# Nine gather buffers for each expert table, in memory shared with the second block's constants

## The chip, the core and the metric

The kernel runs on one core of a Trainium2 chip. The metric is the device time of one execution, in microseconds. The core has a matrix engine (TensorE, PE), a vector engine (VectorE, DVE), an activation engine (ScalarE, ACT), GpSimd (POOL), which here does nothing but issue the gathers, and SyncE (SP), which issues the plain loads. All transfers run on the same 16 DMA engines.

## What is computed

A sequence of 256 tokens and 16 meta tokens, 1024 wide, goes through a first block of two layers, and then through a second block with three attention branches and a feed-forward network. What matters here is the expert layer (`peer`), which each of the first two layers ends with. For every token it picks 128 experts (8 heads, top 16 of each), and every expert is one row of 1024 numbers in each of two tables of 16,384 rows:

```python
u_sel = jnp.take(u, expert, axis=0)
v_sel = jnp.take(v, expert, axis=0)
act = jax.nn.gelu(jnp.einsum('btd,bthkd->bthk', hx, u_sel), approximate=False)
return jnp.einsum('bthk,bthkd->btd', (gate * act).astype(h.dtype), v_sel)
```

The second block's constants (rotary cosines and sines, a swap and a flip matrix, the decay of the retention branch, the bucket and mask rows of the relative bias) come as one array `cs2` of 128 x 3584 numbers.

## The kernel before, in words

Tokens lie on the 128 partitions, in tiles: tile 0, tile 1, and tile 2 with the 16 meta tokens. The expert layer of a tile is a row of **slots**. In slot k every partition (token) gets its k-th expert: GpSimd issues one gather of 128 rows of `peer_u` (L344, 512 KB) and then one of 128 rows of `peer_v` (L349, 512 KB). There are 528 slots: 16 for the meta tokens, in which the eight heads lie on the partitions, and 128 each for tile 0 and tile 1 of the first layer and tile 0 and tile 1 of the second. Number them n = 0 to 527.

What a slot goes through, in order:

- VectorE multiplies the `u` row by the token's row and sums (`dot`, L1435, semaphore `dot`).
- ScalarE takes the gelu of the 128 sums (`gelu`, L932).
- VectorE makes a 128x128 diagonal matrix of gelu times gate (`coef`, L1444, semaphore `diag`, four buffers). In its instruction order it comes two slots behind the dot. It waits until TensorE has done slot n-4.
- TensorE multiplies the diagonal by the `v` row and adds it up in two banks of PSUM (`sums_slot`, L494, four matmul records a slot). It raises the semaphore `vsum`.

A `u` gather of slot n waits in GpSimd's queue until dot n-NU is done, a `v` gather until the sum of slot n-NV is done. NU is 4 and NV is 8. As GpSimd issues u(n), v(n), u(n+1), ... in one queue, a gather that waits holds back all that follow. The buffers lie in one tile `a1` of 12 x 1024 numbers a partition, the `u` buffers in front.

The order of the other work around the slots is written out by hand. `Beside.to(n)` on TensorE, ScalarE and VectorE means: first do the slots up to n, then go on. The tables `PLAN` (the two `front` passes) and `SIDE` say at which slot each piece of other work comes. `topk` finds the experts of a tile (about 230 steps on VectorE) and writes their numbers to `eidx` (L1424), for which GpSimd waits at each tile. The slots of one tile run beside the next tile's projections, attention and top-k:

- slots 16 to 143 (layer 0, tile 0), 228 to about 604 us, beside the rest of the first layer's top-k; from about 400 us nothing else runs but slots (the straight stretch);
- slots 144 to 271, to about 1110 us, beside `front(0)`: projections, attention (`stick`, eight steps), output projection, query projection, top-k;
- slots 272 to 399, to about 1600 us, beside `front(1)`, the same for tile 1;
- slots 400 to 527, to about 1974 us, beside the second block's first steps (`SIDE`): the memory tokens' keys and values, the bias rows (`trev`, `flip`); from about 1740 us nearly nothing but slots.

After the last slot the second block begins (`split_cols_unit`, L652). The matrices `swap` (L747) and `decayed` use `cs2c`, the buffer of `cs2`.

SyncE loads the weights in 270 units of 512 KB into a ring of R = 8, each when the unit eight back has been used. In this queue stand, before, the loads of `cs2c`, `bcG` and `tsb` ahead of unit `wqA`, and, ahead of unit SPLIT0 (the second block's first with the split weights), a wait for the last top-k and the loads of `mem` and of the last gain row.

Of the kernel before, what the change touches and what calls it, by code (L numbers as in the profile page):

```python
# [22 lines left out]
R = 8  # L23
NU = 4
NV = 8
# [53 lines left out]
CS2 = {}  # L79
# [5 lines left out]
NCS2 = _at  # L85


def program(nc, xin, metain, units, cols, cst, cs2, poolm, bc_rows, peer_u, peer_v, mem, rel, out):
# [10 lines left out]
    with ctx:  # L99
        def sb(name, shape, dt=fp32):  # L100
            return ctx.enter_context(nc.sbuf_tensor(name, shape, dt))
# [33 lines left out]
        A1W = (NU + NV) * 1024  # L135
# [11 lines left out]
        vg = a1[:, NU * 1024:A1W].rearrange("p (n d) -> p n d", d=1024)  # L147
# [54 lines left out]
        cs2c = sb("cs2c", [128, NCS2])  # L202
        bcG = sb("bcG", [128, 512])
        tsb = sb("tsb", [128, 32])
        oh2 = sb("rot_tmp", [128, 512])
# [20 lines left out]
        memx = pw  # L226
        up_cv = a2[:, pw_at:pw_at + 1024].rearrange("p (b k t) -> p b k t", b=2, k=2)
# [59 lines left out]
        def _(sp):  # L287
# [9 lines left out]
            for n in range(N_UNITS):  # L297
                if n == U0["wqA"]:
                    sp.dma_start(cs2c[:, :], cs2).then_inc(S("ld_m"), 16)
                    sp.dma_start(bcG[:, :], bc_rows[3:4, 0:512].to_broadcast([128, 512])).then_inc(S("ld_m"), 16)  # L300
                    sp.dma_start(tsb[0:32, 0:8], rel).then_inc(S("ld_m"), 16)
                if n == SPLIT0:

                    sp.wait_ge(S("eidx"), tk_number(1, 1))
                    sp.dma_start(memx[:, :, :], mem.rearrange("(t p) d -> p t d", p=128)).then_inc(S("ld_mem"), 16)
                    sp.dma_start(bcL, bc_rows[4:5, :].to_broadcast([128, D])).then_inc(S("ld_g"), 16)
                if n >= R:
                    sp.wait_ge(S("w_used"), n + 1 - R)
                sp.dma_start(wring[:, n % R, :], units[in_dram[n], :, :]).then_inc(S(f"w{n % R}"), 16)
# [55 lines left out]
        def _(pe):  # L365
# [124 lines left out]
            def sums_slot(P, k, n, vfill):  # L490
                pe.wait_ge(S("diag"), n + 1)
                pe.wait_ge(S(f"v{k % NV}"), vfill)
                for j in range(2):
                    last = nc.tensor.matmul(ps[0:P, 6 + j, :], diag[:, k % 4, 0:P],  # L494
                                            vg[:, k % NV, j * 512:(j + 1) * 512], start=False, stop=False)
                last.then_inc(S("vsum"), 1)
# [224 lines left out]
            nc.tensor.matmul(ps[0:8, 0, 0:384], tsb[0:32, 0:8], cs2c[0:32, CS2["bucket"]:CS2["bucket"] + 384],  # L721
# [7 lines left out]
            for j in range(4):  # L729
                last = nc.tensor.matmul(ps[:, j, :], cs2c[:, CS2["flip"]:CS2["flip"] + 128],  # L730
                                        pw.rearrange("p b n -> p (b n)")[:, j * 512:(j + 1) * 512],
                                        start=True, stop=True)
# [10 lines left out]
            def swap(j):  # L743
                b = 4 + j % 2
                pe.wait_ge(S("iT_ev"), j + 1)
                claim(b)
                nc.tensor.matmul(ps[:, b, 0:256], cs2c[:, 0:128], qkT[:, 8 + j, :], start=True, stop=True)\  # L747
                    .then_inc(S("sw_pe"), 1)
                owe("rot_ps", j + 1, b)
# [138 lines left out]
        def _(act):  # L888
# [212 lines left out]
            squares("nm", lambda t: memx[:, t, :], lambda t: (spare, hn[:, 0, :])[t], [0, 1], 15)  # L1101
# [167 lines left out]
        def _(dve):  # L1269
# [323 lines left out]
            v.tensor_tensor(pw[0:8, 0, 0:384], ps[0:8, 0, 0:384], cs2c[0:8, CS2["future"]:CS2["future"] + 384],  # L1593
# [22 lines left out]
            def rotate(j):  # L1616
# [3 lines left out]
                dve.wait_ge(S("sw_pe"), j + 1)  # L1620
                v.tensor_tensor(tmp, ps[:, 4 + j % 2, 0:256], c2("sin" + k_), ALU.mult).then_inc(S("rot_ps"), 1)
# [321 lines left out]
```

## Time and profile before

| | |
|---|---|
| time, median of 3 runs | 2486.46 us (2483.32 to 2488.86) |
| the profiled execution: time | 2487.36 us |
| the profiled execution: span of the core | 2485.6 us |
| busy: PE, DVE, ACT, POOL | 1982.1, 1413.1, 576.7, 1027.1 us |
| moved by DMA | 707.96 MB, mean 285 GB/s |
| of it the gathers (queue q0) | 553.72 MB, 59.6% of the 16 engines' span |
| mean granted TensorE clock | 0.927 of full speed |

The span is the time from the first to the last instruction, 1.8 us less than the execution's own time. An engine's idle time is put down to what ended it. "issue" is time for which the profile shows no reason; "remote" is an end that it can't assign. The start and end of a GpSimd gather are those of the instruction that writes its descriptors; the data land some us later. The share of DMA is that of busy time over 16 engines, and can come out a little over 1.

### The profile page before, as it was taken

The numbers are of one execution on the slowest core, as the hardware profiler recorded it, in microseconds if no ns is written. First come the engines' busy times: TensorE is split into PE (matmuls) and PEld (weight loads), VectorE is DVE, ScalarE is ACT, GpSimd is POOL, SyncE is SP. The second block draws the span as 40 slices with busy tenths as digits, with TensorE's granted clock in tenths as the row PEclk, the third lists the DMA queues.
The fourth block names the chain that finished last, engine by engine and source line by source line (L and its number), as shares of the span: only waits on it lengthen the run. The fifth ranks groups of instructions, "written<-read, shape, count | busy, mean of one in ns | idle before, by whom it ended". The sixth has DMA issues, their size and how long they took to land.

```text
span 2485.6 us, 21257 instructions
## 1 busy us (share of the span) xinstructions
PE 1982.1 (80%) x6918; PEld 1101.4 (44%) x6918; DVE 1413.1 (57%) x3068; ACT 576.7 (23%) x1204; POOL 1027.1 (41%) x1063
## 2 busy tenths in 40 slices
PE   6756767767898789768877887688877799897998
PEld 3641222222333335423344463243322297676996
DVE  0138788755344554694455447855555455555884
ACT  1111100100112431011134211111100134453663
POOL 0025656766444454464444545656666400000000
PEclk9888989999998889999988899999999899998999
DMA  3257989999889789989966899999999744353653
GB/s 146 85 168 309 371 314 367 369 368 356 320 301 345 272 285 393 348 305 357 396 235 234 329 385 346 343 370 409 396 364 368 284 144 154 111 153 103 187 182 122
DMA packets 194843, 707.96 MB, mean 285 GB/s; under 512 B 21784, under 2 KB 23072, under 8 KB 194480
## 3 DMA queue, kind: packets, MB, share of 16 engines
q0 software_dynamic: 152064, 553.72, 59.6%
q1 hardware_dynamic: 40960, 150.65, 17.9%
q10 hardware_dynamic: 1712, 2.24, 0.3%
q8 instruction: 57, 0.93, 0.2%
q14 instruction: 50, 0.41, 0.0%
HBM read 704.81 MB, written 1.06 MB: 284 GB/s over the span
## 4 chain that ended last, share of the span: by engine, by line
PE 54%; DVE 17%; issue 10%; DMA 7%; POOL 6%; ACT 3%; another core or an unknown queue 1%; ACTq 0%; SPq 0%; DVEq 0%; POOLq 0%
PE ps L494 22%; PE ps L652 15%; DMA a<-in_peer_u,eidx 7%; PE ps L411 5%; PE ps L426 5%; DVE a L1435 4%; POOL a L349 3%; POOL a L344 3%; DVE diag L1444 1%; DVE a L1369 1%; PE ps L444 1%; PE ps L397 1%; PE ps L598 1%; DVE a L1375 1%
## 5 line engine op out<-in xcount | busy, mean ns | idle before, releaser
L494 PE MATMUL ps<-a,diag 128*128 128x512 f32 (+1 forms) x2112 | 1091.9, 657 | 356.2 <-DVE diag L1444 237.2
L494 PEld LDWEIGHTS ps<-a,diag 128*128 128x128 f32 (+1 forms) x2112 | 402.9, 203 | 994.2 <-issue 623.0
L1435 DVE SCALAR_TENSOR_TENSOR a<-a,ps 128x1024 f32<-128x1024 f32 x512 | 622.3, 1216 | 347.3 <-DMA a<-in_peer_u,eidx 289.3
L344 POOL DMA_INDIRECT a<-in_peer_u,eidx x528 | 522.5, 990 | 636.7 <-DVE a L1435 303.4
L349 POOL DMA_INDIRECT a<-in_peer_v,eidx x528 | 503.8, 954 | 303.3 <-issue 133.3
L652 PE MATMUL ps<-a_r 128*128 128x256 f32 (+1 forms) x1648 | 393.8, 332 | 19.9 <-DVE a_r L1583 7.3
L932 ACT ACTIVATE gel<-dots 128x1 f32<-128x1 f32 x528 | 101.1, 201 | 1076.6 <-DVE a L1435 637.9
L652 PEld LDWEIGHTS ps<-a_r 128*128 128x128 f32 x1648 | 279.6, 192 | 52.3 <-DVE a_r L1583 8.1
L1577 DVE TENSOR_TENSOR ring_r<-wring,a_r 128x1024 fp32r<-128x1024 f32 x142 | 173.3, 1222 | 139.8 <-ACT a_r L1091 139.7
L1444 DVE TENSOR_SCALAR diag<-cstc,gel,a 128x128 f32<-128x128 f32 (+1 forms) x528 | 186.1, 354 | 104.0 <-issue 38.9
L1091 ACT ACTIVATE a_r<-wring 128x1024 fp32r<-128x1024 f32 x142 | 149.4, 1053 | 82.3 <-PE ps L652 82.2
L652 PE MATMUL ps<-a_r,ring_r 128*128 128x256 f32 x512 | 144.3, 282 | 0.0
L426 PE MATMUL ps<-xT,wring 128*128 128x128 f32 (+2 forms) x832 | 137.9, 323 | 5.2 <-issue 4.8
L426 PEld LDWEIGHTS ps<-xT,wring 128*128 128x128 f32 x832 | 123.8, 193 | 31.4 <-issue 18.7
L652 PE MATMUL ps<-ring_r,a_r 128*128 128x512 f32 x312 | 125.2, 401 | 0.0
L411 PE MATMUL ps<-wring,xT 128*128 128x512 f32 (+1 forms) x256 | 119.1, 597 | 0.0
L652 PEld LDWEIGHTS ps<-a_r,ring_r 128*128 128x128 f32 x512 | 99.7, 195 | 0.0
L1357 DVE MAX8 a<-a 128x8 f32<-128x128 f32 (+1 forms) x99 | 26.4, 323 | 94.1 <-DMA a<-a 79.2
L411 PEld LDWEIGHTS ps<-wring,xT 128*128 128x128 f32 (+1 forms) x256 | 42.2, 170 | 70.6 <-issue 70.3
L397 PE MATMUL ps<-cstc,hn 128*128 128x128 f32 (+1 forms) x152 | 27.5, 341 | 50.2 <-DVE hn L1302 20.2
L652 PEld LDWEIGHTS ps<-ring_r,a_r 128*128 128x128 f32 x312 | 60.1, 193 | 12.3
L397 PEld LDWEIGHTS ps<-cstc,hn 128*128 128x128 f32 (+1 forms) x152 | 22.7, 186 | 61.6 <-DVE hn L1302 23.9
(218 smaller groups left out, 1299.1 us busy)
## 6 DMA issues: line engine op xcount, KB each, us to landing
wring<-in_units SPq DMA_DIRECT2D x270, 512.0 KB
a<-in_peer_u,eidx POOLq DMA_INDIRECT x528
a<-in_peer_v,eidx POOLq DMA_INDIRECT x528
cs2c<-in_cs SPq DMA_DIRECT2D x1, 1792.0 KB
a<-in_poolm SPq DMA_DIRECT2D x1, 1632.0 KB, 9.2
h<-in_xin SPq DMA_DIRECT2D x2, 512.0 KB, 4.2
bcF<-in_bc_rows SPq DMA_DIRECT2D x2, 512.0 KB, 9.3
a<-in_mem SPq DMA_DIRECT2D x1, 1024.0 KB, 4.9
```

What stands on the lines that cost most here:

```text
L344: g.indirect_dma_start(ug[:, n % NU, :], None, peer_u, bass.IndirectOffsetOnAxis(ap=eidx[:, t, k:k + 1], axis=0))\
L349: g.indirect_dma_start(vg[:, n % NV, :], None, peer_v, bass.IndirectOffsetOnAxis(ap=eidx[:, t, k:k + 1], axis=0))\
L397: last = nc.tensor.transpose(ps2(tb)[:, c * 128:c * 128 + P], src(t)[:, c * 128:(c + 1) * 128], ident[0:P, 0:P])
L411: last = nc.tensor.matmul(ps[0:P, b0 + 2 * n + j, :], lhs(c, c0, P), w[:, j * 512:(j + 1) * 512], start=c == 0, stop=c == chunks - 1)
L426: last = nc.tensor.matmul(ps[:, b, 0:N], w[:, c * 128:(c + 1) * 128], x[:, c, c0:c0 + N], start=c == 0, stop=c == DC - 1)
L494: last = nc.tensor.matmul(ps[0:P, 6 + j, :], diag[:, k % 4, 0:P], vg[:, k % NV, j * 512:(j + 1) * 512], start=False, stop=False)
L652: last = nc.tensor.matmul(dst, a, b, start=start and m == 0, stop=stop and m == 2)
L932: nc.scalar.activation(gel[:, k % 8:k % 8 + 1], dots[:, k % 8:k % 8 + 1], ACT.Gelu)\
L1091: nc.scalar.activation(high(n), wring[:, n % R, :], ACT.Copy).then_inc(S("w_high"), 1)
L1435: v.scalar_tensor_tensor(ug[:, n % NU, :], ug[:, n % NU, :], 1.0, hnm if t == 2 else ps2(4), ALU.mult, ALU.mult, accum_out=dots[:, k % 8:k ...
L1444: v.tensor_scalar(diag[:, k % 4, 0:W], unit_mat, gel[:, k % 8:k % 8 + 1], gate, ALU.mult, ALU.mult).then_inc(S("diag"), 1)
L1577: v.tensor_tensor(low(n), wring[:, n % R, :], high(n), ALU.subtract).then_inc(S("w_low"), 1)
```

## The change

Both rings get nine buffers. The tile `a1` grows from 12 x 1024 to 18 x 1024 numbers a partition. To make room, `cs2c`, `bcG` and the rotation's scratch `oh2`, which had tiles of their own, now lie in `a1`, behind its first 12,288 numbers, where `v` buffers are. So SyncE loads `cs2c` and `bcG` only once the last slot's sum is done, ahead of unit SPLIT0 + 8, with a semaphore `ld_cs` of their own, for which the first `swap` and the first `rotate` wait. The two parts of `cs2` that are needed earlier (`flip`, and `bucket` with `future`) are loaded by two DMAs of their own into the tile `spare`, ahead of unit SPLIT0. The scratch of one squaring moves out of `spare`.

```diff
-NU = 4
-NV = 8
+NU = 9
+NV = 9
...
-        A1W = (NU + NV) * 1024
+        A1W = max((NU + NV) * 1024, 12288 + NCS2 + 1024)
...
-        cs2c = sb("cs2c", [128, NCS2])
-        bcG = sb("bcG", [128, 512])
+        cs2c = a1[:, 12288:12288 + NCS2]
+        bcG = a1[:, 12288 + NCS2:12800 + NCS2]
         tsb = sb("tsb", [128, 32])
-        oh2 = sb("rot_tmp", [128, 512])
+        oh2 = a1[:, 12800 + NCS2:13312 + NCS2]
...
+        flip, bucket, future = spare[:, 0:128], spare[0:32, 128:512], spare[0:8, 512:896]
...
                 if n == U0["wqA"]:
-                    sp.dma_start(cs2c[:, :], cs2).then_inc(S("ld_m"), 16)
-                    sp.dma_start(bcG[:, :], bc_rows[3:4, 0:512].to_broadcast([128, 512])).then_inc(S("ld_m"), 16)
                     sp.dma_start(tsb[0:32, 0:8], rel).then_inc(S("ld_m"), 16)
                 if n == SPLIT0:
...
+                    sp.dma_start(flip, cs2[:, CS2["flip"]:CS2["flip"] + 128]).then_inc(S("ld_m"), 16)
+                    sp.dma_start(spare[:, 128:896], cs2[:, CS2["bucket"]:CS2["bucket"] + 768]).then_inc(S("ld_m"), 16)
+                if n == SPLIT0 + R:
+
+                    sp.wait_ge(S("vsum"), 16 + 4 * SLOTS)
+                    sp.dma_start(cs2c, cs2).then_inc(S("ld_cs"), 16)
+                    sp.dma_start(bcG, bc_rows[3:4, 0:512].to_broadcast([128, 512])).then_inc(S("ld_cs"), 16)
...
             def sums_slot(P, k, n, vfill):
                 pe.wait_ge(S("diag"), n + 1)
-                pe.wait_ge(S(f"v{k % NV}"), vfill)
+                pe.wait_ge(S(f"v{n % NV}"), vfill)
...
             def swap(j):
                 b = 4 + j % 2
+                if j == 0:
+                    pe.wait_ge(S("ld_cs"), 32)
                 pe.wait_ge(S("iT_ev"), j + 1)
...
             act.wait_ge(S("ld_mem"), 16)
-            squares("nm", lambda t: memx[:, t, :], lambda t: (spare, hn[:, 0, :])[t], [0, 1], 15)
+            squares("nm", lambda t: memx[:, t, :], lambda t: (a2[:, SMALL + 4096:SMALL + 5120], hn[:, 0, :])[t], [0, 1], 15)
...
                 dve.wait_ge(S("sw_pe"), j + 1)
+                if j == 0:
+                    dve.wait_ge(S("ld_cs"), 32)
```

The `v` buffer of a slot is now chosen by n instead of by k in the tile; the uses of `cs2c` for `bucket`, `flip` and `future` become uses of the new names.

## Rows read from the trace of the kernel before

**Rows 1.** Waits of GpSimd: line, waited for, us in total, times, longest

```profile
POOL a L344 <- DVE a L1435: 303.4, 111, 18.2
...
POOL a L349 <- PE ps L494: 122.9, 100, 3.4
POOL a L349 <- remote: 47.1, 17, 4.5
```

**Rows 2.** Windows by stage: length, busy (instructions) per engine, PEclk, DMA share, GB/s

```profile
228.00:400.00 172.00, 120.30 (x226) 42.94 (x226) 134.74 (x424) 14.91 (x60) 110.91 (x117) 0.88 0.92 345
400.00:600.00 200.00, 143.38 (x284) 51.27 (x284) 133.19 (x283) 17.13 (x74) 138.59 (x142) 0.97 0.98 371
600.00:1110.00 510.00, 413.06 (x1234) 190.15 (x1232) 281.67 (x658) 107.91 (x239) 251.72 (x257) 0.92 0.87 321
1110.00:1600.00 490.00, 397.03 (x1263) 202.90 (x1264) 279.78 (x643) 110.80 (x234) 250.63 (x255) 0.92 0.88 327
1600.00:1740.00 140.00, 118.59 (x301) 55.15 (x300) 75.39 (x154) 21.85 (x66) 87.20 (x93) 0.96 0.99 385
1740.00:1966.00 226.00, 175.06 (x344) 64.43 (x342) 125.68 (x248) 20.95 (x85) 152.01 (x162) 0.92 0.98 376
```

**Rows 3.** Timeline of GpSimd, 1839 to 1848.5: start, us, instruction, idle before

```profile
1840.12 0.93 POOL L344 DMA_INDIRECT a<-in_peer_u,eidx  x1 [0.30 <-issue]
1845.21 0.99 POOL L349 DMA_INDIRECT a<-in_peer_v,eidx  x1 [4.16 <-remote]
1846.51 0.93 POOL L344 DMA_INDIRECT a<-in_peer_u,eidx  x1 [0.30 <-issue]
```

**Rows 4.** Timeline of VectorE, the same stretch

```profile
1845.05 0.34 DVE L1444 TENSOR_SCALAR diag<-cstc,gel,a 128x128 f32<-128x128 f32 x1 [1.38 <-remote]
```

**Rows 5.** Timeline of TensorE, the same stretch

```profile
1841.44 1.98 PE L494 MATMUL ps<-a,diag 128*128 128x512 f32 x4 [0.59 <-DVE diag L1444]
```

**Rows 6.** Waits of GpSimd, 400 to 600 us

```profile
POOL a L349 <- PE ps L494: 12.0, 13, 3.4
POOL a L349 <- remote: 7.6, 3, 4.5
POOL a L344 <- remote: 3.1, 1, 3.1
```

**Rows 7.** Waits of GpSimd, 1740 to 1966 us

```profile
POOL a L349 <- remote: 19.8, 5, 4.3
POOL a L349 <- PE ps L494: 4.9, 8, 2.8
```

**Rows 8.** Windows before and after one pause of GpSimd

```profile
1820.00:1838.00 18.00, 15.00 (x27) 5.07 (x25) 9.67 (x19) 1.22 (x6) 13.73 (x15) 0.82 1.03 409
1846.00:1850.00 4.00, 3.70 (x10) 1.44 (x9) 2.28 (x6) 0.41 (x2) 3.02 (x4) 1.00 0.78 223
```

**Rows 9.** Timeline of GpSimd, 305 to 324 us

```profile
321.86 0.94 POOL L344 DMA_INDIRECT a<-in_peer_u,eidx  x1 [12.31 <-DVE a L1435]
```

**Rows 10.** Timeline of GpSimd, 603 to 620 us

```profile
614.26 0.94 POOL L344 DMA_INDIRECT a<-in_peer_u,eidx  x1 [2.56 <-DVE a L1435]
```

**Rows 11.** Timeline of VectorE, 610 to 628 us

```profile
622.66 1.22 DVE L1435 SCALAR_TENSOR_TENSOR a<-a,ps 128x1024 f32<-128x1024 f32 x1 [1.93 <-DMA a<-in_peer_u,eidx]
```

**Rows 12.** Timeline of VectorE in an attention step, 1285 to 1326 us

```profile
1300.83 0.95 DVE L1559 TENSOR_TENSOR a<-a,ps 128x768 f32<-128x768 f32 x1 [6.83 <-PE ps L600]
```

**Rows 13.** Timeline of VectorE, 1168 to 1216 us

```profile
1194.10 1.22 DVE L1435 SCALAR_TENSOR_TENSOR a<-a,ps 128x1024 f32<-128x1024 f32 x1 [3.65 <-DMA a<-in_peer_u,eidx]
```

**Rows 14.** Timeline of TensorE, 1970 to 2004 us

```profile
1979.23 1.88 PE L501 MATMUL ps<-h,cstc 128*128 128x512 f32 x4
...
2002.71 0.59 PE L747 MATMUL ps<-a,cs2c 128*128 128x256 f32 x2
```

**Rows 15.** The page, DMA issues: KB each, us to landing

```profile
cs2c<-in_cs SPq DMA_DIRECT2D x1, 1792.0 KB
...
a<-in_mem SPq DMA_DIRECT2D x1, 1024.0 KB, 4.9
```

More of the change, by code:

```diff
@@ L146, in program @@
         ug = a1[:, 0:NU * 1024].rearrange("p (n d) -> p n d", d=1024)
-        vg = a1[:, NU * 1024:A1W].rearrange("p (n d) -> p n d", d=1024)
+        vg = a1[:, NU * 1024:(NU + NV) * 1024].rearrange("p (n d) -> p n d", d=1024)
         a2 = sb("a2", [128, A2W])
@@ L491, in sums_slot @@
                 pe.wait_ge(S("diag"), n + 1)
-                pe.wait_ge(S(f"v{k % NV}"), vfill)
+                pe.wait_ge(S(f"v{n % NV}"), vfill)
                 for j in range(2):
                     last = nc.tensor.matmul(ps[0:P, 6 + j, :], diag[:, k % 4, 0:P],
-                                            vg[:, k % NV, j * 512:(j + 1) * 512], start=False, stop=False)
+                                            vg[:, n % NV, j * 512:(j + 1) * 512], start=False, stop=False)
                 last.then_inc(S("vsum"), 1)
@@ L720, in _ @@
             claim(0)
-            nc.tensor.matmul(ps[0:8, 0, 0:384], tsb[0:32, 0:8], cs2c[0:32, CS2["bucket"]:CS2["bucket"] + 384],
+            nc.tensor.matmul(ps[0:8, 0, 0:384], tsb[0:32, 0:8], bucket,
                              start=True, stop=True).then_inc(S("trev_pe"), 1)
@@ L729, in _ @@
             for j in range(4):
-                last = nc.tensor.matmul(ps[:, j, :], cs2c[:, CS2["flip"]:CS2["flip"] + 128],
+                last = nc.tensor.matmul(ps[:, j, :], flip,
                                         pw.rearrange("p b n -> p (b n)")[:, j * 512:(j + 1) * 512],
@@ L1592, in _ @@
             dve.wait_ge(S("turned"), AT["nm"][3] + 2)
-            v.tensor_tensor(pw[0:8, 0, 0:384], ps[0:8, 0, 0:384], cs2c[0:8, CS2["future"]:CS2["future"] + 384],
+            v.tensor_tensor(pw[0:8, 0, 0:384], ps[0:8, 0, 0:384], future,
                             ALU.add).then_inc(S("trev_sb"), 1)
```

## The prediction, made before the changed kernel was run

> **What bounds the kernel now.** I read the waits of GpSimd first, because the change touches nothing but what GpSimd waits for. Its `u` gathers waited 303.4 us for a dot, its `v` gathers 122.9 us for a sum and 47.1 us for something that the profile calls remote [rows 1]. That is no gain yet: an issuer that waits for a consumer costs time only where the consumer later starves. So I cut the run into stages by windows and asked of each what ends last [rows 2].
>
> From 400 to 600 us and from 1740 to 1966 us nothing runs but slots. No engine is full there except the DMA engines (share 0.98), at 371 and 376 GB/s. GpSimd issued 142 gathers (71 slots) in 200 us, which is 2.82 us a slot, and 162 (81 slots) in 226 us, 2.79 us a slot [rows 2]. From 600 to 1110 and from 1110 to 1600 us a slot takes about 3.9 us (257 and 255 gathers), with TensorE busy 81% of the time and DMA 0.87 and 0.88. There the front's order of projections, attention and top-k sets the pace.
>
> What the reader is to see in the straight stretches is that they are not smooth. Back to back, GpSimd needs 1.24 us a gather (from 1840.12, 0.93 us of work and 0.30 us to the next; the pair at 1845.21 and 1846.51 is 1.30 apart), so 2.48 us a slot. But the `v` gather at 1845.21 stood idle for 4.16 us, released by "remote" [rows 3]. At 1845.05 VectorE's `coef` was released by "remote" too [rows 4]. By the code both wait on `vsum`, here for the same slot: `v` of slot n for n-8, `coef`, four slots behind it, for its own minus 4. TensorE had meanwhile gone on with later sums (the one at 1841.44 started on its diagonal) [rows 5]. So my reading is that TensorE's work is on time, but the news of it comes late, about once in 12 slots. The ring of eight is then just too short. DMA runs at 409 GB/s and 1.03 before such a pause and falls to 223 GB/s and 0.78 after it [rows 8]: it is full only between the pauses. Two gathers (1.049 MB) at 409 GB/s are 2.56 us. That is the floor of a slot by DMA, and 2.48 us that by GpSimd.
>
> **The change part by part.** The profiled execution took 2487.36 us, 0.9 us over the median of the runs shown. The sum is made against it.
>
> *NV 8 to 9.* In a pause GpSimd may issue one `v` and one `u` gather more, so each pause gets shorter by up to 2.48 us, one slot. The `u` ring with nine no longer binds ahead of the `v` ring.
> - 1740 to 1966 us: five remote waits of 19.8 us in all, the longest 4.3, and eight on TensorE of 4.9 us, the longest 2.8; 0.3 us of each is the usual step [rows 7]. Five times 2.48 is 12.4 us, and the one long wait among the eight gives 2.4: 14.8 us. Bound by rate: 81 slots at 2.60 us (between floor and a rest of each pause) are 211 us, 15 less than 226. I take 14.
> - 400 to 600 us: 13 waits of 12.0 us, three of 7.6 and one of 3.1 [rows 6]; less 0.3 each that is 17.6 us, of which the four longest keep about 4 in all, and some of the short ones are taken up anyway. I take 11. Bound by rate: 71 slots at 2.60 are 185 us, 15 less than 200.
> - 1600 to 1740 us: DMA is at 385 GB/s and 0.99 [rows 2]. At 409 the same bytes would take 132 us, 8 less. But other work (memory keys, norms) sets a part of it. I take 2.
>
> *NU 4 to 9.* Where VectorE is away from the slots for more than four of them, the `u` ring runs full.
> - At 321.86 GpSimd had been idle 12.31 us [rows 9]. With nine and nine it could issue seven gathers more (8.7 us) before the `v` ring stops it. As `v` then waits for the first sum after VectorE's return, I count 4.9 us of lead. Together with short pauses before 400 us, a lead that can last is limited by the `v` ring to some 8 us. I take 7. It is all paid out in the straight stretch behind it.
> - At 614.26 it had been idle 2.56 us [rows 10], and the last dot ahead of the next tile's norm then waited 1.93 us for its data [rows 11]. The norm starts `front(0)`. I take 2.
> - 600 to 1600 us else: in attention VectorE waits 6.83 us for TensorE's chain with its buffers full [rows 12], and in top-k VectorE itself is the bound. The projections leave the diagonals made ahead of TensorE. One dot on the path waits 3.65 us for data, at 1194.10 [rows 13], ahead of the norm of `front(1)`; a copy and a transpose stand behind it, so I take 1.5 of it. Bounds: 0 and 10 us.
>
> *`cs2c` moved behind the last slot.* The last sum ends just ahead of 1979.23, the first `swap` starts at 2002.71 [rows 14]: 23 us. The load is 1792 KB and the row of `bcG` 256 KB. `mem`, 1024 KB, landed in 4.9 us [rows 15], so 2048 KB at that pace take 9.8 us, or 5.1 us at 409 GB/s with the queue's start added. The gathers are done by then. It is hidden by TensorE's last norm and three split units; without that cover it would cost 7 to 10 us. Behind the waiting SyncE stands unit SPLIT0 + 8, which waits for the second split unit anyway, and so later. Cost 0. What it takes away at 787 us (2 MB, 5 us of DMA) lay beside TensorE-bound work: 0, bound 0 to 3.
>
> *The two small loads ahead of SPLIT0.* 64 KB and 384 KB more in a stage at 0.99: 0.46 MB at 409 GB/s is 1.1 us lost. The new waits on `ld_cs`, the moved scratch and the index by n: 0, as the loads are done and nothing is added to an engine's work.
>
> Sum: 14 + 11 + 2 + 7 + 2 + 1.5 - 1.1 = 36.4 us. 2487.36 - 36.4 = 2451.0 us.
>
> **A rule against the change.** The windows show 409 GB/s with the share at 1.03 [rows 8], so the DMA engines can give 9% more than the 376 of the straight stretch. The Trainium skill ("DMA: Bandwidth & Descriptors", section Specifications) says that the memory behind one core limits it to about 358 GB/s. By that rule the straight stretches would be past their limit already and deeper rings worth nothing there. The trace here disagrees, with 409; I go by the trace.
>
> **Rivals.**
> - *The pauses stay.* What holds `vsum` back could last until the DMA backlog is worked off, or scale with it, so that the ring only fills one slot further and the pause ends as late against the data as before. For it: I can't name the cause, and the profile calls it remote. Against it: both waiting engines are released at one moment while TensorE works on. Then only the `u` part is left: 7 + 2 + 1.5 + 2 - 1.1 = 11.4, so 2476 us. It decides if the waits called remote keep their length of about 4 us.
> - *Full already.* The share of 0.98 means what it says, and the dips are made up by the fuller time between. For it: 0.98 and 0.99 in three windows [rows 2]. Against it: 0.78 after a pause [rows 8]. The time would be 2487 us.
> - *More than one slot.* The longer `u` lead also takes up the rest of each pause and the slots reach GpSimd's floor of 2.48: 152 slots times (2.80 - 2.50) is 46 us instead of the 25 counted, and 7 more before 400 us. The time would be 2451 - 21 - 7 = 2423 us.
> - *Slower.* More gathers in flight stand ahead of everything else on the 16 engines. If what TensorE needs (its instructions, its news) comes later by as much as the ring is longer, VectorE, whose diagonals have still four buffers, starves: 528 / 12 = 44 pauses, each longer by 2.48 us and not covered in, say, half of them (slots are the bound there), is +55 us, less the 11 of above: 2531 us. It is a loss as soon as a pause grows by more than 0.5 us in those 22. For it: VectorE was held by the same pause [rows 4]. Against it: only 1.38 us, then it catches up.
>
> **How the numbers follow.** My forecast, 2440 to 2466, 0.54. Pauses stay, 2470 to 2482, 0.19. More than one slot, 2415 to 2440, 0.08. Full already, within 0.2% (5 us, about what a measurement of this kernel can tell from no change), 0.10. Slower by more, 0.09. Faster is 0.54 + 0.19 + 0.08 = 0.81. The range reaches from 2430 to 2480: it holds my case with the outer terms (0 and 10 for the middle, 8 for 1600 to 1740 us), most of the pauses-stay case and about half of "more", some 0.76 to 0.8 in all; it leaves out no change and slower.
>
> **What the profile after would show.** GpSimd's waits for a dot in slots nearly gone, and those for a sum grown, since the `v` ring now binds everywhere. The waits called remote at about 1.5 us instead of 4. In the two straight stretches 2.60 us a slot and some 400 GB/s, with the share at 1.0 or over. The wait of 12.31 us at about 4. The top-k stages and the attention steps unchanged in length. The first `swap` right behind the third split unit, with no wait for `ld_cs`. I am wrong if a remote wait is still 4 us long, if slots in the straight stretches stay at 2.8, or if TensorE waits ahead of `swap`.

## The result: 1.1% slower, and not on every chip

The changed kernel took 2512.99 us (median of four runs, 2510.03 to 2515.26), the kernel before 2484.89 us on the same chip (2481.65 to 2488.86). The ratio is 1.0112, 95% interval 1.0092 to 1.0132: 28 us slower. The forecast was 2451 us, 36 us faster.

The waits of GpSimd after, the answer to [rows 1]:

```profile
POOL a L355 <- PE ps L500: 415.7, 167, 14.2
...
POOL a L355 <- remote: 51.8, 17, 4.8
POOL a L350 <- DVE a L1443: 7.3, 24, 0.3
```

The waits for a dot are gone (303.4 to 7.3 us), as foretold. The waits of the `v` gathers called remote are not shorter: 17 of them before and after, 47.1 and 51.8 us. (Six of the `u` gathers, 10.3 us in all, are gone.) The windows by stage, beside [rows 2]:

```profile
228.00:400.00 172.00, 111.55 (x202) 40.88 (x203) 125.55 (x401) 13.77 (x54) 104.92 (x111) 0.81 0.90 336
400.00:600.00 200.00, 146.72 (x293) 55.75 (x291) 136.59 (x300) 17.68 (x76) 137.56 (x140) 0.94 0.97 368
600.00:1110.00 510.00, 411.68 (x1230) 189.92 (x1231) 269.05 (x645) 107.70 (x238) 249.41 (x261) 0.91 0.87 319
1110.00:1600.00 490.00, 381.75 (x1248) 196.87 (x1246) 267.93 (x624) 106.79 (x226) 237.03 (x247) 0.92 0.84 316
1600.00:1740.00 140.00, 114.44 (x290) 55.30 (x290) 87.84 (x163) 19.55 (x62) 84.64 (x87) 0.94 0.92 356
1740.00:1966.00 226.00, 171.67 (x353) 65.51 (x351) 126.54 (x250) 25.61 (x91) 151.31 (x161) 0.94 0.99 381
```

In the straight stretches GpSimd issues as many gathers as before (140 for 142, 161 for 162), so nothing was won there. The loss lies in the first and the fourth window: of the same work, less is done in the same time (51 slots' dots begun for 56, and 124 for 127), and the DMA share fell. The third holds one too, at the tile turn, as shown below. The fifth looks like a loss too, but it doesn't show the same work: at 1600 us the changed kernel is eight slots behind. Counted by slots, 396 to 446 took 148.9 us before and 148.1 after. A pause in the straight stretch, beside [rows 3] (timeline of GpSimd; between the two it issued without a stop):

```profile
1813.70 0.99 POOL L355 DMA_INDIRECT a<-in_peer_v,eidx  x1 [4.55 <-remote]
...
1850.57 0.99 POOL L355 DMA_INDIRECT a<-in_peer_v,eidx  x1 [4.77 <-remote]
```

The loss begins in the first slots of the first tile. Timelines of GpSimd, ScalarE, VectorE and TensorE there:

```profile
230.34 0.93 POOL L350 DMA_INDIRECT a<-in_peer_u,eidx  x1 [15.99 <-DVE eidx L1432]
...
260.18 0.94 POOL L350 DMA_INDIRECT a<-in_peer_u,eidx  x1 [0.30 <-issue]
269.45 0.94 POOL L355 DMA_INDIRECT a<-in_peer_v,eidx  x1 [8.34 <-PE ps L500]
```

```profile
253.47 0.20 ACT L940 ACTIVATE gel<-dots 128x1 f32<-128x1 f32 x1 [7.84 <-remote]
264.67 0.20 ACT L940 ACTIVATE gel<-dots 128x1 f32<-128x1 f32 x1 [11.00 <-remote]
```

```profile
249.91 0.29 DVE L1377 MATCH_REPLACE8 a<-a 128x128 f32<-128x128 f32 x1 [0.69 <-issue]
...
251.31 0.29 DVE L1377 MATCH_REPLACE8 a<-a 128x128 f32<-128x128 f32 x1 [1.11 <-issue]
252.71 0.09 DVE L1377 MATCH_VALUE_LOAD a<-a 128x8 f32 x1 [1.11 <-issue]
```

```profile
254.89 3.78 PE L500 MATMUL ps<-a,diag 128*128 128x512 f32 x4 [5.28 <-remote]
265.40 6.86 PE L500 MATMUL ps<-a,diag 128*128 128x512 f32 x11 [6.73 <-remote]
```

GpSimd issues 25 gathers back to back, from 230.34 to 261.12. From about 248 on VectorE starts instructions of 0.1 to 0.3 us only every 0.7 or 1.4 us, with nothing to wait for, and ScalarE and TensorE wait 8, 11, 5 and 7 us for remote events. All go on between 264.6 and 265.4, 3.5 us and more after GpSimd's last issue has ended. I call this a hold. Then GpSimd itself had to wait 8.34 us for a sum. In [rows 3] and [rows 4] it had the same end: GpSimd's last issue ended at 1841.05, and the others went on at 1845.05, 4.0 us later.

Before, GpSimd had stopped after 16 gathers here, because the ring of four was full, and ScalarE went on after 6.53 us. GpSimd and ScalarE of the kernel before:

```profile
249.99 0.94 POOL L344 DMA_INDIRECT a<-in_peer_u,eidx  x1 [2.41 <-issue]
```

```profile
249.75 0.20 ACT L932 ACTIVATE gel<-dots 128x1 f32<-128x1 f32 x1 [6.53 <-issue]
```

Now GpSimd ran for 25 gathers, and the other engines stood for longer. The same at the tile turn: GpSimd issued 24 gathers up to 629.7 us, and then waited 8.02 us. ScalarE's copy of the finished sums waited 19.31 us (11.34 before), and TensorE, which clears the banks of the sums behind it, 14.19 us (1.21 before). GpSimd, ScalarE and TensorE after:

```profile
637.73 0.94 POOL L355 DMA_INDIRECT a<-in_peer_v,eidx  x1 [8.02 <-PE ps L500]
```

```profile
631.86 1.02 ACT L953 ACTIVATE h<-ps 128x1024 f32<-128x1024 f32 x1 [19.31 <-remote]
```

```profile
633.03 1.01 PE L494 MATMUL ps<-zb 128*128 128x512 bf16 x2 [14.19 <-issue]
```

And at the start of `front(1)`, where TensorE's first expert sums behind its transposes waited 5.20 us before (first line) and 15.29 us after:

```profile
1138.87 3.78 PE L494 MATMUL ps<-a,diag 128*128 128x512 f32 x4 [5.20 <-DVE diag L1444]
```

```profile
1165.26 3.78 PE L500 MATMUL ps<-a,diag 128*128 128x512 f32 x4 [15.29 <-DVE diag L1452]
```

The wait of [rows 9], 12.31 us, did get shorter, to 3.11 us:

```profile
322.79 0.94 POOL L355 DMA_INDIRECT a<-in_peer_v,eidx  x1 [3.11 <-issue]
```

The lower granted clock (0.918 in the profiled run, 0.927 before) is not the cause: a matmul of the sums took 656 ns on average for 657.

And in all of VectorE's waits:

```profile
DVE a L1443 <- DMA a<-in_peer_u,eidx: 145.7, 116, 4.0
...
DVE diag L1452 <- issue: 87.9, 27, 13.1
...
DVE diag L1452 <- PE ps L500: 69.0, 33, 4.3
...
DVE diag L1452 <- remote: 46.5, 16, 5.2
```

The dots wait for their data half as long as before (291.4 us then). What was won there is paid at `diag`: VectorE stood idle ahead of it for 236.7 us in all, and for 103.9 before. ScalarE's waits changed little: its longest in attention (L1073) came to 122.9 us for 107.1.

The moved load is no part of it. From the page's DMA issues, and from TensorE's timeline (the first `swap`, which no idle time precedes):

```profile
a<-in_cs SPq DMA_DIRECT2D x1, 1792.0 KB, 7.0
```

```profile
2029.37 0.59 PE L755 MATMUL ps<-a 128*128 128x256 f32 x2
```

### The profile page after: what moved, and what is told of

It reads as the page before. It is cut to its first block, busy times and chain, and to the rows that moved or that the text cites. A ratio compares the mean times of both kernels' runs of the same rounds, so it can differ in the third digit from the quotient of the medians.

```text
span 2512.6 us, 21260 instructions
## 1 busy us (share of the span) xinstructions
PE 1972.4 (78%) x6918; PEld 1106.5 (44%) x6918; DVE 1407.9 (56%) x3068; ACT 576.1 (23%) x1204; POOL 1019.2 (41%) x1063
## 4 chain that ended last, share of the span: by engine, by line
PE 55%; DVE 17%; issue 10%; POOL 5%; DMA 4%; another core or an unknown queue 4%; ACT 4%; ACTq 0%; SPq 0%; DVEq 0%; POOLq 0%
PE ps L500 22%; PE ps L658 15%; PE ps L417 5%; PE ps L432 5%; DVE a L1443 5%; DMA a<-in_peer_u,eidx 4%; POOL a L355 3%; POOL a L350 3%; DVE diag L1452 1%; PE ps L450 1%; PE ps L403 1%; DVE a L1377 1%; DVE a L1383 1%; PE ps L588 1%
## 5 line engine op out<-in xcount | busy, mean ns | idle before, releaser
L500 PEld LDWEIGHTS ps<-a,diag 128*128 128x128 f32 (+1 forms) x2112 | 409.2, 205 | 997.4 <-issue 629.8
L350 POOL DMA_INDIRECT a<-in_peer_u,eidx x528 | 510.3, 966 | 373.5 <-DVE eidx L1432 213.7
L1549 DVE SCALAR_TENSOR_TENSOR a<-ps,cstc 128x512 f32<-128x512 f32 (+1 forms) x16 | 13.2, 825 | 79.8 <-PE ps L588 36.4
```

Of the source, the lines that this page charges most:

```text
L350: g.indirect_dma_start(ug[:, n % NU, :], None, peer_u, bass.IndirectOffsetOnAxis(ap=eidx[:, t, k:k + 1], axis=0))\
```

## The experiments

They ran on several chips, of two kinds. On three, before took 2425 to 2427 us (four comparisons) and no trace has a wait for a remote event: I call them quiet. On three others before took 2491 to 2494 us (three comparisons), and every trace of them has 51 to 70 such waits, as the first pair had 61 and 70. One of the quiet chips ran two comparisons, 9 minutes apart, and was quiet in both; each other chip was used once, so whether the kind belongs to the chip or to the moment isn't known. Each kernel is compared with before on its own chip.

### Each part of the change alone (quiet chip)

Variants of the changed kernel. `rings_4_8` has its memory and its loads, with the old rings:

```diff
-NU = 9
-NV = 9
+NU = 4
+NV = 8
```

`rings_9_8` and `rings_4_9` change one of the two lines; the memory keeps its size. `lead_4_8` keeps nine and nine buffers and takes back the lead:

```diff
-                if n >= NU:
-                    g.wait_ge(S("dot"), n + 1 - NU)
+                if n >= 4:
+                    g.wait_ge(S("dot"), n + 1 - 4)
...
-                if n >= NV:
-                    g.wait_ge(S("vsum"), n + 1 - NV)
+                if n >= 8:
+                    g.wait_ge(S("vsum"), n + 1 - 8)
```

> Everything of the change stays (shared memory, the two small loads, the moved loads of cs2c and bcG with the waits for them), but the rings hold 4 and 8 buffers again. Theory A (the longer lead of GpSimd causes the loss: it issues longer without a pause, and the other engines are held up meanwhile): the time of before, 2485 us within 5. Rival B (the shared memory, the moved loads or their waits cost it): the time of the changed kernel, 2513 us within 5. The prediction on record put this part at 1.1 us of cost.

> The changed kernel with nine buffers for u and eight for v. Theory A (lead of GpSimd; the short ring of u was what made it pause): most of the loss is here already, 2505 to 2515 us. Rival C (the ninth buffer of v is what hurts, since a pause now has to wait for sums that are further behind): back to 2485 us or, with the 7, 2 and 1.5 us that the prediction gave to the longer ring of u, 2475.

> The changed kernel with four buffers for u and nine for v. Theory A: the short ring of u still makes GpSimd pause, so about the time of before, 2480 to 2490 us; the prediction's own reading (pauses come from the ring of v being one slot too short) gives 27 us less than before here, 2458. Rival C (the ninth buffer of v hurts): 2505 to 2515 us.

> The changed kernel with nine and nine buffers in its memory, but GpSimd waits as before: for the dot of four slots back and for the sum of eight slots back. Theory A (the lead, not the buffers): 2485 us within 5. Rival D (which addresses the gathers write and how many distinct buffers they go round): 2513 us within 5. Rival B also gives 2513.

`changed_again` is the changed kernel itself. `diag_7` has seven buffers for `diag`, indexed by n, and `coef` waits for the sum of seven slots back.

> The changed kernel itself, beside the kernel before on the chip of this comparison. In the first four experiments the kernel before took 2427 us, 58 us less than in the comparison of the result, and the trace of the kernel with rings of four and eight had no wait of GpSimd for a remote event, where that of before had 17 (47 us). Theory E (the loss of 28 us needs a chip on which the news of the other engines is held up; without the hold the change gains a little through the longer ring of u, as nine and eight did with 8 us): 2414 to 2422 us here, ratio 0.995 to 0.998. Theory F (the ninth buffer of v costs by itself, on any chip): 2440 us or more, ratio 1.005 or more.

> The changed kernel with seven buffers for diag in place of four, so that VectorE can scale three slots further ahead of the sums. Theory E: where nothing is held up the four buffers are no limit, so within 4 us of the changed kernel. Rival G (VectorE starves on its four diagonals as soon as GpSimd runs ahead; the slower case of the prediction): 10 us or more faster than the changed kernel of this call.

| kernel | us | before | ratio, 95% interval |
|---|---|---|---|
| rings_4_8 | 2427.38 | 2426.77 | 1.0003 [0.9994, 1.0012] |
| lead_4_8 | 2428.53 | 2426.77 | 1.0009 [1.0000, 1.0018] |
| rings_4_9 | 2425.94 | 2426.77 | 0.9999 [0.9990, 1.0008] |
| rings_9_8 | 2418.84 | 2426.77 | 0.9971 [0.9959, 0.9982] |
| changed_again | 2417.26 | 2425.45 | 0.9961 [0.9947, 0.9974] |
| diag_7 | 2414.93 | 2425.45 | 0.9952 [0.9938, 0.9966] |

On a quiet chip the change gains 8 us, nearly all of it by the longer ring of `u`. The ninth buffer of `v` alone gives nothing, and the memory and the loads cost nothing. With the lead taken back the gain is gone. `diag_7` is the fastest, but can't be told from the changed kernel. The expectations of the first four runs rested on the first chip and missed, because this chip has no holds; those of `changed_again` (theory E) and `diag_7` (no limit here) came true. Rival G is refuted for quiet chips only. The changed kernel's first slots on it (VectorE; ahead of them GpSimd issues back to back as on the first chip), and two windows:

```profile
250.40 0.28 DVE L1377 MATCH_REPLACE8 a<-a 128x128 f32<-128x128 f32 x1
250.59 0.08 DVE L1377 MATCH_VALUE_LOAD a<-a 128x8 f32 x1
250.66 0.28 DVE L1377 MATCH_REPLACE8 a<-a 128x128 f32<-128x128 f32 x1
...
252.63 0.67 DVE L1383 MAX8 a<-a 128x8 f32<-128x128 f32 x3
```

```profile
228.00:400.00 172.00, 129.89 (x252) 45.55 (x254) 149.63 (x470) 16.30 (x66) 125.16 (x132) 0.92 0.99 389
400.00:600.00 200.00, 150.41 (x317) 55.03 (x317) 141.29 (x284) 24.74 (x88) 149.03 (x153) 0.97 1.02 403
```

153 gathers in 200 us are 2.61 us a slot, next to the 2.56 to 2.60 that the prediction worked out. It takes no longer ring: the dots of slots 60 to 136 come 2.62 us apart in `rings_4_8` and 2.59 in `changed_again`, those of 460 to 527 2.56 and 2.59. A longer run of GpSimd does no harm here, so a long run by itself is not enough for a hold. The Trainium skill ("DMA: Bandwidth & Descriptors", section Specifications) puts the memory's limit for one core at about 358 GB/s; this trace disagrees with it over a whole stage, with 403.

### What a pause costs (another quiet chip)

```diff
+                if n >= 16 and n % 12 == 4:
+                    g.wait_ge(S(f"v{(n - 2) % NV}"), 16 * ((n - 2) // NV + 1))
```

stands ahead of the gather of `u` in the changed kernel (`pause_9_9`) and with rings of four and eight (`pause_4_8`). In `landed_4` the wait stands in every slot from the fourth, for n - 4.

> The changed kernel with a pause of GpSimd put in by force: in every twelfth slot it waits until the gather of v of two slots back has landed. Issued back to back that gather is 3.7 us old and lands at 7.9, so each of the 43 pauses is about 4.2 us, the length that the prediction found on the first chip. The prediction's reading (in a stretch bound by transfers a pause costs its length less what the ring's lead gives back): the pauses outside the attention stretches and the gaps count in part, 30 to 100 us more than the changed kernel, and less here than with rings of four and eight. Rival J (gathers already issued keep the queue full through a pause of 4 us): within 10 us of the changed kernel.

> The same forced pauses in the changed kernel with rings of four and eight. If the longer rings let GpSimd make up for a pause, as the prediction said (2.48 us a pause), this one is slower than the pauses with nine and nine by 40 to 100 us more than the 8 us that part them without pauses. If rival J holds, both pairs differ by the same 8 us, and this takes 2427 to 2437 us.

> The changed kernel, where GpSimd also waits, ahead of each slot, until the gather of v of four slots back has landed. It bounds the gathers under way, and where news is held up it makes GpSimd stop soon. On a chip without held news (before 2427 us): a slot takes GpSimd 2.48 us of issuing or more, so four slots are 10 us, and a gather lands 7.9 us after its issue (median, rings of four and eight): nothing is waited for, the time of the changed kernel within 4 us (2417). On a chip with held news (before 2485 us): theory H (the long run of issues without a stop is what makes the hold long) gives back 20 us or more of the 28; rival (the loss has nothing to do with how far GpSimd runs) gives 2513.

Before took 2426.35 us. `pause_9_9` took 2490.34 (ratio 1.0257 [1.0240, 1.0274]), `pause_4_8` 2498.33 (1.0303 [1.0286, 1.0320]), `landed_4` 2418.00 (0.9961 [0.9949, 0.9974]). So 43 pauses of some 4 us cost 72 and 71 us with either rings, measured against 2418 and 2427: 1.7 us each on average. The 8 us between the rings stay what they were, so the 40 to 100 us that the longer rings were to save here didn't appear, as rival J said; its other half, that the queue covers a pause, is refuted. One such pause (timeline of GpSimd), and the window that answers to [rows 2]:

```profile
434.76 0.93 POOL L357 DMA_INDIRECT a<-in_peer_v,eidx  x1 [0.30 <-issue]
440.00 0.94 POOL L352 DMA_INDIRECT a<-in_peer_u,eidx  x1 [4.31 <-DMA a<-in_peer_v,eidx]
```

```profile
400.00:600.00 200.00, 140.01 (x274) 49.19 (x274) 130.94 (x276) 16.87 (x72) 133.42 (x136) 0.97 0.95 357
```

Pauses of this length once in 12 slots bring a quiet chip close to the rate of the first one (136 gathers for 142, 357 GB/s for 371). `landed_4` shows that four slots between issue and landing are enough.

### Holds by force (a chip with holds)

VectorE's dot waits, at nine slots of the first straight stretch and five of the last, for a gather that GpSimd issues later:

```diff
+                if n % 12 == 4 and (28 <= n <= 124 or 460 <= n <= 508):
+                    dve.wait_ge(S(f"v{(n + 2) % NV}"), 16 * ((n + 2) // NV + 1))
```

`hold2_4_8` has rings of four and eight, `hold2_9_9` the changed ones. `hold5_9_9` has n + 5 for n + 2.

> A hold of VectorE's news is put in by force at 14 slots of the straight stretches: the dot of slot n waits until the gather of v of slot n+2 has landed. Rings of four and eight in the changed kernel's memory, so GpSimd stops at u of slot n+4 until that dot is done, about 4.2 us after its last issue, as the traces of the first chip show it. A forced pause cost 1.7 us over all stretches (43 of them, 73 us); in the stretches bound by transfers I expect 2 to 4 us each: 2427 + 28 to 56 = 2455 to 2483 us.

> The same hold (dot of slot n until v of slot n+2 has landed) with nine and nine buffers. It ends at the same moment of the stream of gathers whatever GpSimd does, and GpSimd can issue on through it. This is the hold that the prediction assumed: its step (the longer ring shortens the pause) gives nearly no cost, 2417 to 2427 us. If it costs as much as with four and eight, the ring can't help even there.

> Nine and nine buffers, and the dot of slot n waits until v of slot n+5 has landed: GpSimd runs on to u of slot n+7, where the sums of slot n-2 stop it, and the hold ends about 4.2 us after its last issue. This is a hold that ends only when GpSimd stops (theory H). Theory H: the pause is back at full length, and the engines behind the dots stand still for three slots more, so 30 to 80 us above the changed kernel (2447 to 2497), and against its own base it costs as much as hold of two with four and eight, or more. Rival K (with longer rings the engines catch up from the buffered rows, and the gathers lose nothing): within 10 us of the changed kernel.

Before took 2493.84 us. `hold2_4_8`: 2530.90, ratio 1.0147 [1.0123, 1.0171]. `hold2_9_9`: 2518.19, 1.0108 [1.0078, 1.0138]. `hold5_9_9`: 2595.59, 1.0400 [1.0371, 1.0430]. By the ratio of the result the changed kernel itself would take about 2522 here (it did not run on this chip), so 14 holds that end at a fixed moment cost nine and nine nothing, and four and eight 37 us, 2.6 each. Holds that last longer, in which GpSimd runs out of buffers, cost nine and nine some 74 us. The traces agree: in the two stretches with forced holds `hold2_9_9` is within 1 us of after, `hold2_4_8` 36.8 us above before, and `hold5_9_9` 63.5 us above after (4.5 a hold). As the chip has holds of its own, these are net costs. The expectations, written for a quiet chip, came true as differences (28 to 56, none, 30 to 80 us); rival K is refuted.

The pair `hold2_9_9` and `hold2_4_8` also shows the change where nothing was forced, with the same memory and loads in both. From the traces, the start of the dot of a slot (the 528 dots counted in order); each column is how much longer the stretch takes in the first kernel than in the second, us. Front A and B are `front(0)` and `front(1)`; the tile turn is where the slots pass from one tile to the next.

| slots | after - before | hold2_9_9 - hold2_4_8 | before - rings_4_8 (quiet) | after - changed_again (quiet) | pause_9_9 - changed_again (both quiet) | pause_9_9_b - pause_9_9 (quiet) |
|---|---|---|---|---|---|---|
| 16 to 28 | +8.4 | +4.4 | +3.1 | +11.5 | +2.3 | +8.9 |
| 28 to 136, straight | -5.2 | -24.0 (forced) | +25.0 | +25.9 | +33.1 | +0.5 |
| 136 to 152, tile turn | +7.5 | +6.3 | +6.2 | +14.3 | +5.6 | +10.6 |
| 152 to 272, front A | +3.7 | +4.0 | +4.4 | +6.0 | -0.6 | +16.2 |
| 272 to 280, front B starts | +9.8 | +9.7 | +2.4 | +12.3 | 0.0 | +0.2 |
| 280 to 344 | +6.9 | +10.6 | +4.9 | +8.6 | 0.0 | +15.5 |
| 344 to 440 | -7.5 | -9.1 | +2.7 | +0.3 | +11.9 | +4.4 |
| 440 to 527, straight | +1.4 | -17.1 (forced) | +15.6 | +17.1 | +24.0 | -0.3 |

How far a row can be trusted is seen where two traces have the same rings. On quiet chips `changed_c` and `changed_again` differ by at most 0.9 us in a row, `rings_4_8_b` and `rings_4_8` by 0.7, but 1.4 in front A and 3.3 in 280 to 344. On chips with holds `landed_4_c` and after (the same rings, a wait more) differ by at most 0.8, but 6.6 in 344 to 440 and 3.7 in the last row; `hold2_4_8` and before by at most 1.8 in the unforced rows, but 6.1 in 16 to 28. The first two columns agree outside the forced stretches: the same sign in each row, at most 4.0 us apart, in sum +28.8 and +25.9. So on a chip with holds the rings make the loss, and the memory and the loads don't.

The third and fourth column show what the holds cost either kernel, against the same rings on a quiet chip: in the straight stretches the same (25.0 and 25.9, 15.6 and 17.1), which is the gain that didn't come; at the starts (16 to 28, 136 to 152, 272 to 280) 12 us with the short rings and 38 with the long ones.

The -5.2 of the first column is no gain of the straight stretch: it lies in slots 28 to 46 (60.6 us before, 55.7 after), where the engines catch up on rows that came during the first hold. Slots 60 to 136 took 213.1 and 211.9 us.

The start of front B shows what makes the difference. GpSimd begins to issue there at slot 272, and stops when a ring is full or a forced pause comes. All traces with holds, and three without:

| kernel | holds | gathers issued before the first stop | TensorE's wait ahead of the first sums behind its transposes, us |
|---|---|---|---|
| pause_9_9_b | yes | 16 | 2.78 |
| before | yes | 20 | 5.20 |
| hold2_4_8 | yes | 20 | 5.67 |
| after | yes | 25 | 15.29 |
| hold2_9_9 | yes | 25 | 15.03 |
| landed_4_c | yes | 25 | 15.10 |
| hold5_9_9 | yes | 25 | 15.45 |
| pause_9_9 | no | 16 | 2.78 |
| rings_4_8 | no | 20 | 2.78 |
| changed_again | no | 29 | 2.78 |

With holds the wait grows with the run of GpSimd, and with a run of 16 it is that of a quiet chip; without holds the run doesn't matter. So here the longer run that the longer rings allow makes the longer hold. (`landed_4_c` and `pause_9_9_b` come in the next section.)

### Other quiet and other held chips

`changed_c`, `rings_4_8_b`, `rings_9_8_b` and `landed_4_b` are kernels of above, meant for a chip with holds; the chip was quiet.

> The changed kernel, as the measure of this call. Where before takes about 2490 us: 1.011 times that (28 us more). Where it takes 2426: 8 us less.

> The changed kernel with rings of four and eight. Theory H (a long run of GpSimd makes the holds long, and the short ring of u ends it): the time of before within 5 us on either kind of chip. Rival B (the memory or the moved loads make the loss where news is held up): the time of the changed kernel.

> The changed kernel with nine and eight buffers. Theory H, on a chip with held news (before 2490 us): most of the loss comes with the long ring of u, so 15 to 28 us above before. Rival C (the ninth buffer of v makes the loss): 2480 to 2490 us. On a chip without: 8 us below before, as in the first experiments.

> The changed kernel, where GpSimd also waits ahead of each slot until the gather of v of four slots back has landed. Theory H, on a chip with held news: a landing's news is held up too, so GpSimd stops after four slots at the latest, the hold ends, and the time is that of before or below, 2470 to 2495 us. Rival L (what counts is only that rows sit in the ring, or how much memory is written): no change against the changed kernel, 2518. On a chip without: the changed kernel within 4 us.

Before took 2425.79 us; the ratios were 0.9960 [0.9949, 0.9971], 1.0000 [0.9991, 1.0010], 0.9978 [0.9969, 0.9988] and 0.9975 [0.9965, 0.9984]. They confirm the quiet side and say nothing on holds.

`landed_4_c` then ran on a chip with holds.

> The changed kernel, where GpSimd also waits ahead of each slot until the gather of v of four slots back has landed. Where before takes about 2490 us: theory H gives the time of before or below, 2470 to 2495 us; the rival, that a landing's news is not held up and so doesn't stop GpSimd, or that its run is not what matters, gives 1.011 times before, 2518. Where before takes 2426: the changed kernel within 4 us, as twice before.

It took 2523.77 us beside 2491.30, ratio 1.0125 [1.0099, 1.0151]: the loss of the changed kernel, whole, as the rival said, and not the 2470 to 2495 of theory H. The first slots again, GpSimd and ScalarE:

```profile
258.19 0.94 POOL L352 DMA_INDIRECT a<-in_peer_u,eidx  x1 [0.30 <-issue]
266.97 0.94 POOL L357 DMA_INDIRECT a<-in_peer_v,eidx  x1 [7.84 <-PE ps L502]
```

```profile
262.97 0.20 ACT L942 ACTIVATE gel<-dots 128x1 f32<-128x1 f32 x1 [10.99 <-remote]
```

GpSimd issued 25 gathers from 227.89 on, all but one of them 1.24 us or so apart, each slot after the landing of four slots back. So news of landings reaches GpSimd through a hold, which theory H had taken to be held up too. And the number of gathers under way, bounded here to four slots as the short ring of `u` bounds it, is not what makes the loss. This kernel left the run as long as it was, so it didn't test the run.

`pause_9_9_b` is `pause_9_9` on a chip with holds, and does cut the run.

> The changed kernel with GpSimd paused in every twelfth slot until the gather of v of two slots back has landed, about 4.2 us each; 2490 us where nothing is held up. Where before takes about 2490 us and the changed kernel 2518: if the holds come from long runs of GpSimd (theory H), the 43 pauses stand in the place of the holds, and the time is 2490 to 2530 us. If the holds come whatever GpSimd does, both costs add up: 2518 + 73 = 2591 us, 2570 or more. Where before takes 2426: 2490 us again.

It took 2549.60 us beside 2492.94, ratio 1.0242 [1.0210, 1.0274]: between the two expectations. The last columns of the table part it. In the straight stretches a held chip now takes as long as a quiet one (+0.5 and -0.3, where it was +25.9 and +17.1 without forced pauses). There the forced pauses stand in the place of the holds, as theory H said. At the start of front B, where a pause cut GpSimd's run from 25 gathers to 16, the loss is gone (+0.2, where it was +12.3). In the first slots and at the tile turn GpSimd had issued 23 and 24 gathers before its first stop, about as many as in the changed kernel (25 and 24), so the +8.9 and +10.6 there say nothing against it. In the fronts themselves the pauses don't replace the holds (+16.2, +15.5, where it was +6.0 and +8.6), and there theory H is not borne out by this kernel. Its waits of GpSimd, all of the run:

```profile
POOL a L352 <- DMA a<-in_peer_v,eidx: 138.0, 29, 14.9
...
POOL a L357 <- remote: 24.4, 9, 4.2
```

## Why the prediction was wrong

- **The step that failed** is "NV 8 to 9. In a pause GpSimd may issue one `v` and one `u` gather more, so each pause gets shorter by up to 2.48 us, one slot", 14 + 11 of the 36.4 us. Of [rows 3 to 5] it took that the news of the sums is late by a fixed time. The trace after shows 17 pauses as before, of 3.0 us on average for 2.8. The long ones in the straight stretches were 4.1 to 4.5 us, behind runs of 22 to 26 gathers; after, they were 4.0 to 4.8 us, behind runs of 24 to 30 (once 56). So the hold ended about 4 us after GpSimd stopped, and the pause moves to the end of the longer run and keeps its length. Measured: nothing gained in either straight stretch. That the news was late was read rightly: around [rows 3 to 5] four sums ended from 1835.73 to 1843.42, and the trace records four updates of their semaphore within 0.2 us, from 1844.95 on. `hold2_9_9` shows that the arithmetic was right for a hold with a fixed end; the premise wasn't.
- **The sign** came from the rival "Slower": longer holds, with VectorE starving. It had 0.09, a price of 2531 us, and as mechanism more gathers in flight. The time was 2513. What it named (a pause that grows with the ring) happened, in the first slots, at the tile turn and in the fronts, where ScalarE and TensorE stand still for 5 to 19 us. Gathers in flight as its cause fall with `landed_4_c`; the four diagonals were not tested on a chip with holds.
- **NU 4 to 9**, 7 + 2 + 1.5 us: about right in sum where nothing is held up (7.9 and 6.9 us, `rings_9_8` and `rings_9_8_b`), and a loss where news is held. The idle 12.31 us of [rows 9] did shrink to 3.11, as foretold. The 2.56 us of [rows 10], at slot 148, and a wait of 6.07 us six slots on gave way to one of 8.02 at slot 153; on a quiet chip the two are 1.70 and 6.81 us with the old rings, and both are gone with the new ones.
- **`cs2c` moved, two small loads**, 0 and 1.1 us: right. 1792 KB landed in 7.0 us ahead of a `swap` without a wait, and `rings_4_8` is at 1.0003. (The 5.1 us in that term is the bytes at 409 GB/s alone, with no start added.)
- **1600 to 1740 us**, 2 us of gain: 0.8 us by slots (396 to 446), no more than two traces of one kernel differ; on a quiet chip `changed_again` is 5 us faster there than `rings_4_8`.
- **The signs named for being wrong** were the right ones: remote waits of 4 us and 2.8 us a slot. That the top-k and attention steps keep their length was not: from slot 280 to 344 the kernel took 6.9 us more, from 344 to 440 7.5 less.
- **Full already** (2487 us) and **More than one slot** (2423 us) don't hold either: a quiet chip does a slot in 2.56 to 2.62 us with the old rings (2.80 with holds), so the dips were not made up, and in no run did the slots of a straight stretch come faster than 2.56 us, the floor that the prediction gave to DMA.
- **Pauses stay** (2476 us) described the straight stretches rightly, but left out that the engines behind a longer hold have no cover elsewhere.

Shown: the rings make the loss, and only where there are holds; at the start of front B it comes with the length of GpSimd's run, in seven traces; a pause by force replaces the holds in the straight stretches; landings are not held. Argued only: that the run's length also makes the longer holds in the first slots and at the tile turn, where no forced pause cut it. Unexplained: the fronts, and what a hold is. Not run where there are holds: `rings_4_8`, `rings_9_8`, `rings_4_9` and `diag_7` as they are, so which of the two rings makes the loss, and whether more diagonals would lessen it, is open.

Open as well: what differs between the chips, and a rival stands here that no run settles. The recording itself may have a part in the holds. Every timed run carries a span and clock as well, so no run is known to have gone without it. And the traces with holds are those that lack records: 12,820 to 13,744 landings are in them for 21,782 to 21,785 in the quiet ones, and from 400 to 600 us, where the gathers are dense, a quarter (618 after, 2460 in `changed_again`). The page then gives no time to landing for the gathers, as these two lines show, the first after, the second `changed_again`:

```profile
a<-in_peer_u,eidx POOLq DMA_INDIRECT x528
```

```profile
a<-in_peer_u,eidx POOLq DMA_INDIRECT x528, 9.1
```

With records missing, the word "remote" alone proves little; the idle times rest on the starts and ends of instructions, and the total on the time of the run. The Trainium skill ("NOTIFIC — the notification-queue block", section 7.1 Overflow: three behaviours, one of which stalls the engine) says that the block which writes the records of a trace holds back the engines that produce them when its internal queues fill. No run here shows its state, and nothing above rests on it.

## What to carry to other kernels

Before a wait is priced by how much a longer buffer would shorten it, find out what ends it: a moment of its own, or the stop of the engine that waits. In the first case one more buffer is worth one slot; in the second the pause only moves, and a short ring was what kept it short (TensorE's wait of 5 us and not 15 at the start of front B). Where a gain rests on a wait for a remote event, measure it on more than one chip: this change is worth 8 us on one kind and costs 28 on the other. And compare stages by the same work, not by the same time: a window at a fixed time slides over other slots once the kernel is late.

## What was not expected of the hardware

- Two kinds of chips, 2.7% apart with the same kernel (2426 and 2492 us), told apart in the profile by waits for remote events and by the granted clock (0.94 and 0.93).
- In a hold VectorE doesn't stop, it starts short instructions 0.7 or 1.4 us apart, while GpSimd goes on issuing every 1.24 us and the DMA engines run full: 411 GB/s from 246 to 265 us after, and 410 in the same stretch of `changed_again`, where nothing was held.
- A pause of GpSimd of 4 us in a stretch bound by transfers costs 3.4 to 3.7 us (33.1 us for nine, 24.0 for seven, on a quiet chip), and nothing from slot 152 to 344 (-0.6 to 0.0).
- Holds don't add to pauses: forced ones that cost 57 us in the two straight stretches of a quiet chip left a chip with holds there no slower than that quiet one.
- Whether a chip has holds can be told from how many landings its trace holds: 37 to 41% of them are missing, or at most three of 21,785.
